# The last expert products of a 32-expert block joined by column halves, and the closing normalisation put in an order by token half

## The reference, cut to what matters

```python
y = act @ w_down[e] + b_down[e]                      # per expert
yx[token] += gate[token, e] * y[slot of token]       # "combine"
...
x = x + g2 * rms_norm(yx, norm_ffn_post)
# rms_norm(x, g) = x * rsqrt(mean(x*x, axis=-1) + 1e-6) * g
```

## Time and profile before

| what | us |
|---|---|
| median of three executions | 1554.74 |
| the three executions | 1554.74, 1554.3, 1559.04 |
| span of the profiled execution | 1553.9 |
| PE busy in it | 1508.0 |

### The profile page before, as it was taken

How to read it: one execution, slowest core, us unless ns; L and a number is a source line. 1 busy time by engine, 2 the same in 40 slices (tenths; PEclk the granted TensorE clock), 3 DMA queues, 4 the chain that set the end, 5 groups by cost and what they waited for, 6 DMA issues and landing times.

```text
span 1553.9 us, 18202 instructions
## 1 busy us (share of the span) xinstructions
PE 1508.0 (97%) x7044; PEld 836.7 (54%) x7044; DVE 464.1 (30%) x894; ACT 322.4 (21%) x662; POOL 22.3 (1%) x43
## 2 busy tenths in 40 slices
PE   9999999999999999999999899999989999999997
PEld 8667888888888755443333243333324443333332
DVE  3564125665642343512121121212111212121212
ACT  2343142111112443311011011101101111110111
POOL 0000000000000000000000000000000000000000
PEclk9999999999999999999999999999999999999999
DMA  9625444777752255799999999999999999999996
GB/s 388 269 108 195 157 166 163 271 273 268 272 189 59 105 217 203 298 390 429 428 429 429 429 418 424 428 427 429 428 429 427 408 429 428 420 428 428 429 428 278
DMA packets 46142, 513.48 MB, mean 330 GB/s; under 512 B 5200, under 2 KB 5216, under 8 KB 8064
## 3 DMA queue, kind: packets, MB, share of 16 engines
q1 hardware_dynamic: 41408, 482.53, 75.7%
q0 software_dynamic: 4672, 30.06, 5.2%
HBM read 511.51 MB, written 1.06 MB: 330 GB/s over the span
## 4 chain that ended last, share of the span: by engine, by line
PE 82%; DMA 13%; DVE 2%; ACT 1%; issue 1%; SPq 0%; DVEq 0%; ACTq 0%
PE bank L1348 32%; PE bank L724 13%; PE bank L983 9%; DMA ring<-in_up_w 6%; PE bank L992 5%; DMA ring<-in_gate_w 5%; PE bank L1312 3%; PE bank L1380 3%; PE bank L1471 3%; PE bank L1198 2%; PE bank L834 2%; PE bank L1365 2%; DMA ring<-in_down_w 2%; PE bank L1151 1%; PE bank L1140 1%
## 5 line engine op out<-in xcount | busy, mean ns | idle before, releaser
L1348 PE MATMUL bank<-ring,probs_slab 128*64 128x512 f32 x2840 | 640.2, 598 | 23.8 <-DMA ring<-in_gate_w 12.3
L1348 PEld LDWEIGHTS bank<-ring,probs_slab 128*64 128x64 f32 x2840 | 194.9, 137 | 400.9 <-issue 364.1
L983 PE MATMUL bank<-normed,ring 128*128 128x256 f32 x672 | 146.9, 379 | 0.0
L2569 DVE TENSOR_TENSOR mixed_slab<-bank,squares 128x512 f32<-128x512 f32 x31 | 21.4, 692 | 417.9 <-PE bank L1365 417.8
L983 PEld LDWEIGHTS bank<-normed,ring 128*128 128x128 f32 x672 | 127.6, 190 | 18.0 <-issue 0.8
L724 PE MATMUL bank<-normed,ring 128*128 128x256 f32 x384 | 84.5, 381 | 0.4 <-ACT normed L1633 0.4
L724 PEld LDWEIGHTS bank<-normed,ring 128*128 128x128 f32 x384 | 72.2, 190 | 11.7 <-ACT normed L1633 1.2
L992 PE MATMUL bank<-big_slab,ring 128*128 128x256 f32 x352 | 77.6, 379 | 0.0
L992 PEld LDWEIGHTS bank<-big_slab,ring 128*128 128x128 f32 x352 | 66.9, 190 | 9.0
L2577 DVE TENSOR_TENSOR mixed_slab<-bank,squares 128x512 f32<-128x512 f32 x31 | 21.4, 691 | 157.6 <-PE bank L1365 157.6
L1961 ACT ACTIVATE mixed_slab<-bank 128x512 f32<-128x512 f32 x31 | 18.5, 597 | 225.9 <-PE bank L1348 225.9
(11 more groups left out here) (394 smaller groups left out, 1293.0 us busy)
## 6 DMA issues: line engine op xcount, KB each, us to landing
ring<-in_down_w SPq DMA_DIRECT2D x61, 2048.0 KB, 19.8
ring<-in_gate_w SPq DMA_DIRECT2D x60, 2048.0 KB, 18.7
ring<-in_up_w SPq DMA_DIRECT2D x60, 2048.0 KB, 19.2
ring<-in_front_w SPq DMA_DIRECT2D x72, 1024.0 KB, 5.4
held_slab<-in_mod_w POOLq DMA_DIRECT2D x6, 1024.0 KB, 8.8
memory_slab<-in_mod_w POOLq DMA_DIRECT2D x6, 1024.0 KB, 8.7
cross_keys_slab<-in_mod_w POOLq DMA_DIRECT2D x6, 1024.0 KB, 7.3
probs_turned_slab<-in_mod_w POOLq DMA_DIRECT2D x6, 1024.0 KB, 7.7
```

Source lines behind the costliest of these rows:

```text
L983: mm = pe.matmul(bank[bank_at][:, half * T:(half + 1) * T], w[:, (half * DC + k) * P:(half * DC + k + 1) * P], H[:, k, :], start=(k == 0), ...
L1348: mm = pe.matmul(to[half * SLOTS:(half + 1) * SLOTS, :], tokens(k), weights[:, half * D + i * HALF:half * D + (i + 1) * HALF], start=(k == ...
```

## The change

On PE, `combine` of the expert before the last is split into two calls of a new function `combine_half`. The call for half 0 stays in its place, the one for half 1 goes behind the last down product. `last_combine(0)` goes between chunks 1 and 2 of `last_down(1)`. ACT's copies of the two last banks go to `gate_n` and `up_n`, since `down_n` is still to be read, and the two semaphores change places.

In the tail, DVE does the gain of `bank0`, then of `bank2`, as soon as PE is done with them, then `bank3` and last `bank1`. ACT's squares come in the order `bank0`, `bank1`, root of t 0, `bank2`, `bank3`, root of t 1; those of `bank0`, `bank2` and `bank3` wait for DVE, and DVE's gain of `bank1` waits for ACT. `final` is called once for each half, and `mean_base(1)` stands between two of them.

```diff
+            def combine_half(done, half):
+                pe.wait_ge(s_down_n, done)
+                pe.wait_ge(s_gtev, done)
+                of = slice(half * SLOTS, (half + 1) * SLOTS)
+                for t in range(2):
+                    mm = pe.matmul(total[2 * t + half][:, :], GT[of, t * P:(t + 1) * P],
+                                   down_n[of, :], start=False, stop=True, skip_group_check=True)
+                    if half == 1:
+                        mm.then_inc(s_comb, 1)
...
             last_down(0, range(2))
-            combine(EXPERTS - 1)
+            combine_half(EXPERTS - 1, 0)
             last_down(0, range(2, 4))
-            last_down(1, range(4))
+            last_down(1, range(2))
             pe.wait_ge(s_gtev, EXPERTS)
             last_combine(0)
+            last_down(1, range(2, 4))
+            combine_half(EXPERTS - 1, 1)
             last_combine(1)
...
+            dve.wait_ge(s_half_comb, n * 2 + 1)
             out_gained(0, 0)
+            dve.wait_ge(s_half_comb, n * 2 + 2)
+            out_gained(1, 0)
             mean_base(0)
-            out_gained(1, 0)
+            dve.wait_ge(s_comb, n * 2 + 2 * EXPERTS)
+            out_gained(1, 1)
+            dve.wait_ge(s_out_sq, 2)
+            out_gained(0, 1)
+            dve.wait_ge(s_out_gain, 4)
+            final(0, 0)
             mean_base(1)
-            out_gained(0, 1)
-            final(0)
-            out_gained(1, 1)
-            final(1)
+            final(0, 1)
+            final(1, 0)
+            final(1, 1)
```

More of the change, by code:

```diff
@@ L1403, in last_down @@
                         mm.then_inc(s_half_down, 1)
+            def combine_half(done, half):
[7 more added lines that the diff above has]
+                        mm.then_inc(s_comb, 1)
             def last_combine(half):
-                of = (down_n, gate_n)[half]
-                pe.wait_ge((s_down_n, s_half_n)[half], (EXPERTS, 1)[half])
+                of = (gate_n, up_n)[half]
+                pe.wait_ge((s_half_n, s_down_n)[half], (1, EXPERTS)[half])
                 for t in range(2):
@@ L2009, in _ @@
             act.wait_ge(s_half_down, 1)
-            act.activation(down_n, bank_up[:, :], ACT.Copy).then_inc(s_down_n, 1)
+            act.activation(gate_n, bank_up[:, :], ACT.Copy).then_inc(s_half_n, 1)
             load_table(ACT.Sqrt)
             act.wait_ge(s_chunk, EXPERT_CHUNKS)
-            act.activation(gate_n, bank_down[:, :], ACT.Copy).then_inc(s_half_n, 1)
+            act.activation(up_n, bank_down[:, :], ACT.Copy).then_inc(s_down_n, 1)
             act.wait_ge(s_router, 3)
@@ L2023, in out_squares @@
             def out_squares(t, half):
-                act.activation(sig_f, total[2 * t + half][:, :], ACT.Square,
+                act.activation(flat(MIX2, 0), total[2 * t + half][:, :], ACT.Square,
                                accum_out=stats[:, 70 + 2 * t + half:71 + 2 * t + half]).then_inc(s_out_sq, 1)
[L2027 to L2036, removed]
+                act.wait_ge(s_out_sq, 2 * t + half + 1)
+            act.wait_ge(s_out_gain, 1)
+            out_squares(0, 0)
+            act.wait_ge(s_comb, n * 2 + (2 * EXPERTS - 1))
+            out_squares(0, 1)
+            act.wait_ge(s_out_base, 1)
+            mean_root(71, 84, 74, s_root)
+            act.wait_ge(s_out_gain, 2)
+            out_squares(1, 0)
+            act.wait_ge(s_out_gain, 3)
+            out_squares(1, 1)
+            act.wait_ge(s_out_base, 2)
+            mean_root(73, 85, 75, s_root)
         @block.vector
@@ L2736, in out_gained, with final @@
                 at = slice(half * HALF, (half + 1) * HALF)
-                dve.wait_ge(s_out_sq, 2 * half + t + 1)
                 dve.tensor_tensor(UTOK[:, t, at], total[2 * t + half][:, :], out_gain[:, at],
                                   MUL).then_inc(s_out_gain, 1)
-                dve.wait_ge(s_out_gain, 2 * half + t + 1)
             def mean_base(t):
-                dve.wait_ge(s_out_sq, t + 1)
+                dve.wait_ge(s_out_sq, 2 * t + 1)
                 dve.tensor_scalar(stats[:, 84 + t:85 + t], stats[:, 70 + 2 * t:71 + 2 * t], 1.0 / D, EPS,
                                   MUL, ADD).then_inc(s_out_base, 1)
[L2748 to L2755, removed]
+            def final(t, half):
+                if half == 0:
+                    step(rstd(74 + t, s_root, t))
+                at = slice(half * HALF, (half + 1) * HALF)
+                dve.scalar_tensor_tensor(out=UTOK[:, t, at], in0=UTOK[:, t, at],
+                                         scalar=stats[:, 74 + t:75 + t], in1=XTOK[:, t, at],
+                                         op0=MUL, op1=ADD).then_inc(s_final, 1)
+            dve.wait_ge(s_half_comb, n * 2 + 1)
             out_gained(0, 0)
+            dve.wait_ge(s_half_comb, n * 2 + 2)
+            out_gained(1, 0)
             mean_base(0)
-            out_gained(1, 0)
+            dve.wait_ge(s_comb, n * 2 + 2 * EXPERTS)
[4 more added lines that the diff above has]
+            final(0, 0)
             mean_base(1)
-            out_gained(0, 1)
-            final(0)
-            out_gained(1, 1)
-            final(1)
+            final(0, 1)
+            final(1, 0)
+            final(1, 1)
 def constants():
```

## The result

| | before | changed |
|---|---|---|
| median of 22 executions each, us | 1555.51 | 1558.34 |
| span of the profiled execution | 1553.9 | 1556.9 |
| first `last_down` product to last weight load on PE | 11.76 | 14.02 |
| from there to the end of DVE's last row | 5.51 | 5.57 |
| closing stretch (sum of the two) | 17.27 | 19.59 |

The ratio is 1.0014, 95% interval 1.0008 to 1.002: slower by 2.2 us (1.2 to 3.1), and within the 0.3% that the prediction called no change. The forecast was 2.5 more, 1557.2 us, and the median came out at 1558.34.

What follows compares the result with a forecast made beforehand. Last 20 us: bound by PE up to its last product, then by DVE. 1.72 + 0.51 + 0.14 + 0.14 = 2.51 on 1554.74 gave 1557.2 us; own range 1556.4 to 1558, 8 in 10 1554.8 to 1559.3.

Steps and rivals of the forecast that it cites:

- The passes: PE's two combine_half calls: 64-row passes of one half share no step, four steps of 0.43 each; +1.72 us.
- The switches: PE's closing products: three more changes of form at 0.17 each; +0.51 us, from 0.42 to 0.60.
- Waits on PE: PE's closing products: no wait ended or added; copies of the last banks stay covered, about 0.7 if uncovered.
- The prediction's opening: Expert stage: last expert's down weights land up to 1530.19; from there no transfer stands in the chain.
- The tail: DVE after PE's last product: start 0.14 later relative to PE, run 4.73 instead of 4.59; +0.14 and +0.14 us.
- The sum: Closing stretch: 1.72 + 0.51 + 0.14 + 0.14 = 2.51 us more, median 1557.2 us.
- The lower edge of the range: Whole kernel: 1556.4 us, said to hold with switches free for one and no tail term.
- A: PE's 64-row passes overlap after all or are priced by rows; 0.8 left, 1555.5 us; chance 0.14.
- B: Closing stretch: the new order saves what it costs; at best 0.34 more, 1555.1 us, no change; chance 0.08.
- C: DVE stalls at its new wait before bank3's gain; 4.9 more, 1559.6 us, slower by over 0.3%; chance 0.09.
- D: Closing stretch: faster by over 0.3%, 4.7 us, with no mechanism seen; chance 0.03.

Runs made afterwards that it cites:

- e7: Changed kernel with the split combine's four products dealt out by token half, so each place has both partition halves; last row 17.90, ratio 1.0003.
- e5: Kernel before with the one combine between the last down products ordered half 0, 0, 1, 1; last row 17.27, ratio 0.9995.
- e6: Kernel before with the product order half 0, 0, 1, 1 in all 30 such combines; last row 17.27, ratio 0.9998.
- e3: Changed kernel with the combine left whole in its old place, last_combine(0) still between the down chunks; last row 18.45, ratio 1.001.
- e4: Changed kernel with all last down products first, then the whole combine, then both last_combine calls; last row 18.24, ratio 1.0009.
- e1: Changed kernel with PE in the order of before, only the ACT and DVE tail changed; last row 17.34, ratio 0.9995.
- e8: Changed kernel with PE as before and gains in the order bank0, bank2, bank1, bank3; last row 16.99, ratio 0.9997.

## Why the prediction was right

**The passes (+1.72 forecast).** Right in size: 1.70 by the changed kernel against e7. The price of a lone 64-row pass, taken from the earlier trace rows, is 0.43 in the changed trace. Right also that nothing shares a step with two products of one half between 128-row groups. Wrong was the sentence that a step carries two passes "only where neighbours lie on different partition halves": e5 and e6 have such products two apart in the list, and they share all the same. The order of halves costs PE no time; what costs is that the change parted the two halves, by 7.37 us of work on all 128 rows. For this kernel both readings gave the same number, so the sum came out right without having tested that sentence, and only e5 parted them.

**The switches (+0.51).** 0.56 by e7 against before, 0.19 each.

**Waits on PE (none).** Right; the changed kernel has none. That the cover was needed is shown by e3, with 0.70 us. The prediction's opening reads the last expert's down weights as landed by 1530.19, the end of the last transfer in the chain. They were not all there: the DMA share was 1.00 and 1.01 until 1537.97, and e4, which reads the last ones sooner, waited for them twice. The sum needed only that they had landed by 1540, which it says too.

**The tail (+0.28).** Mis-sized: it measured +0.06, by 5.57 against 5.51 from the last weight load to the end of the last row. DVE's later start, forecast 15.05 behind the first product, was at 15.07 and so right. The run from there was forecast at 4.73 and took 4.52. Two gains in a row went to the reciprocal in 1.32 and not 1.43 (the second starts 0.61 behind the first and not 0.70), `mean_base(1)` took 0.07 and not 0.10, and the row behind it made way for the reciprocal after 0.65 and not 0.72: I had taken the spacings at which instructions of different kinds follow each other, some of them behind a wait, for a run of equal ones. Together with the start this makes 19.59 and not 19.8. ACT's second root was ready 0.19 us before DVE asked for it, by the trace, where the prediction had 0.4 to spare.

**The sum.** 2.32 us in the closing stretch against 2.51; 2.2 (1.2 to 3.1) by the times. The median lies 1.1 above the forecast, and 0.8 of that is the median of before, which came out at 1555.51 over 22 executions where the three shown had given 1554.74. Two statements beside the sum do not hold. The lower edge of the range, 1556.4, does not follow from its own terms: 1.72 and the 0.34 of two switches give 1556.8. And 22 executions of each kernel tell 2.2 us from nothing, less than half of the 4.7 us that the prediction gave as about what a measurement can tell.

**The rivals.** A (passes priced by rows) is refuted by the single loads 0.43 apart, B with it. C (a stall at DVE's new wait) did not come: DVE's gain follows PE's release, and the closing stretch has no idle time in it. D did not either.

## What to carry to other kernels

Products that fill half of the array are free only in company: before such a group is split, ask whether each place still holds work for both partition halves. Each change of form that is added costs too, 0.19 us here. Where an engine list ends in a chain, take the banks in the order in which they are finished rather than hold an engine for the last one (0.35 us between e1 and e8 in their traces, too little for the times), and look which small copy loses its cover when products are moved.

## What was not expected of the hardware

TensorE let 64-row products of one partition half run beside those of the other though two products, four passes, stood ahead of them in the program: eight passes in 1.92 us in both orders, in each of the 30 groups (20.7 us of weight loads in all before, 21.2 in e6). The increments still arrived in the order of the program, the first of them 0.86 us later than before. How far ahead it looks was not tried. In the changed kernel 7.37 us of 128-row work lie between the two halves (1538.58 to 1545.95), and nothing was shared across it. Whether a single such product would end the sharing, or the waits for semaphores that stand there as well, or only the distance, was not tried either.
